# Second feed-forward's first projection by seven half-size products a chunk, with the seventh product's sum on GpSimd

## The reference

```python
def swiglu(h, w_in, w_out):
    gate, up = jnp.split(h @ w_in, 2, axis=-1)
    return ((jax.nn.silu(gate) * up) @ w_out).astype(h.dtype)
...
        h = h + swiglu(rms_norm(h, ffn_norm[i]), ffn_w_in[i], ffn_w_out[i])
    h = rms_norm(h, final_norm)
```

## Time and profile before

| | |
|---|---|
| median of 3 runs | 1679.61 us (1678.21 to 1684.54) |
| span of the profiled execution | 1680.7 us |
| the profiled execution's own time | not given apart from its span |
| TensorE busy | 1640.0 us, 98% |
| TensorE weight loads busy | 1333.0 us, 79% |
| VectorE busy | 919.1 us, 55% |
| ScalarE busy | 632.4 us, 38% |
| GpSimd busy | 92.6 us, 6% |
| chunks 1 to 21 of the second up-projection | about 1316 to 1545 us |
| down-projection behind it | about 1545 to 1666 us |

### The profile page before, as it was taken

How to read it: one execution, slowest core, us unless ns; L and a number is a source line. 1 busy time by engine, 2 the same in 40 slices (tenths; PEclk the granted TensorE clock), 3 DMA queues, 4 the chain that set the end, 5 groups by cost and what they waited for, 6 DMA issues and landing times.

```text
span 1680.7 us, 20208 instructions
## 1 busy us (share of the span) xinstructions
PE 1640.0 (98%) x7941; PEld 1333.0 (79%) x7941; DVE 919.1 (55%) x1262; ACT 632.4 (38%) x816; POOL 92.6 (6%) x130
## 2 busy tenths in 40 slices
PE   8999999999999999999999999999999999999997
PEld 3588777878887888888888789977768888888885
DVE  5665686677667654444444574145766544444323
ACT  2352458432233343333332533146653332223221
POOL 0100000111010000000000100003420000000000
PEclk9899999999999999999999999999999999999998
DMA  9432101755444233332234221224442333332331
GB/s 320 129 119 80 44 26 51 226 164 179 160 150 151 64 102 85 101 101 77 86 103 131 86 76 52 76 65 96 97 127 75 101 100 101 100 90 66 92 104 51
DMA packets 227365, 176.71 MB, mean 105 GB/s; under 512 B 15812, under 2 KB 213316, under 8 KB 227270
## 3 DMA queue, kind: packets, MB, share of 16 engines
q1 hardware_dynamic: 220662, 151.23, 30.9%
q0 software_dynamic: 6608, 24.19, 4.4%
HBM read 166.84 MB, written 2.13 MB: 101 GB/s over the span
## 4 chain that ended last, share of the span: by engine, by line
PE 83%; DVE 9%; ACT 4%; issue 1%; SPq 1%; DMA 1%; DVEq 0%; POOLq 0%; POOL 0%; ACTq 0%
PE PS L477 23%; PE PS L479 23%; PE PS L478 23%; PE PS L2393 2%; PE PS L486 1%; DVE WL L92 1%; DVE T L92 1%; DMA MODW<-in_w_mod 1%; PE PS L498 1%; PE PS L500 1%; PE PS L499 1%; SPq L2682 1%; PE PS L649 1%; ACT WH L88 1%; DVE SUMS L111 1%
## 5 line engine op out<-in xcount | busy, mean ns | idle before, releaser
L477 PE MATMUL PS<-XH,WH 128*128 128x512 f32 (+2 forms) x1264 | 481.1, 381 | 3.2 <-DVE WL L92 1.1
L478 PE MATMUL PS<-XL,WH 128*128 128x512 f32 (+2 forms) x1264 | 476.8, 377 | 0.0
L479 PE MATMUL PS<-XH,WL 128*128 128x512 f32 (+2 forms) x1264 | 476.8, 377 | 0.0
L92 DVE TENSOR_TENSOR WL<-WS,WH 128x2048 fp32r<-128x2048 f32 (+3 forms) x131 | 272.8, 2083 | 209.4 <-ACT WH L88 206.6
L477 PEld LDWEIGHTS PS<-XH,WH 128*128 128x128 f32 (+1 forms) x1264 | 236.0, 187 | 48.9 <-DVE WL L92 2.0
L479 PEld LDWEIGHTS PS<-XH,WL 128*128 128x128 f32 (+1 forms) x1264 | 235.9, 187 | 44.8
L478 PEld LDWEIGHTS PS<-XL,WH 128*128 128x128 f32 (+1 forms) x1264 | 236.0, 187 | 43.2 <-issue 0.7
L88 ACT ACTIVATE WH<-WS 128x2048 fp32r<-128x2048 f32 (+3 forms) x131 | 229.1, 1749 | 76.2 <-PE PS L479 46.7
L477 PE MATMUL PS<-HH,WH 128*128 128x512 f32 x352 | 137.2, 390 | 0.2 <-DVE WL L92 0.2
L478 PE MATMUL PS<-HL,WH 128*128 128x512 f32 x352 | 136.9, 389 | 0.0
L479 PE MATMUL PS<-HH,WL 128*128 128x512 f32 x352 | 136.9, 389 | 0.0
(11 more groups left out here) (373 smaller groups left out, 2294.7 us busy)
## 6 DMA issues: line engine op xcount, KB each, us to landing
WS<-in_w_in SPq DMA_DIRECT2D x24, 1024.0 KB, 5.4
WS<-in_ffn_w_up SPq DMA_DIRECT2D x44, 512.0 KB, 4.9
WS<-in_ffn_w_in SPq DMA_DIRECT2D x44, 512.0 KB, 4.8
MSRC<-in_w_mod POOLq DMA_DIRECT2D x32, 512.0 KB, 4.9
WS<-in_fox_w_in SPq DMA_DIRECT2D x16, 1024.0 KB, 5.6
WS<-in_ffn_w_down SPq DMA_DIRECT2D x16, 704.0 KB, 4.5
WS<-in_ffn_w_out SPq DMA_DIRECT2D x16, 704.0 KB, 4.5
MODW<-in_w_mod SPq DMA_DIRECT2D x8, 1024.0 KB, 11.7
```

What stands on the lines that cost most here:

```text
L92: self.e.tensor_tensor(o, a, b, op).then_inc(*self.done.to(*key))
L477: e.matmul(o, lh, rh, start=first and i == 0, stop=False)
L478: e.matmul(o, lh, rl, start=False, stop=False)
L479: ins = e.matmul(o, ll, rh, start=False, stop=last and i == n - 1)
```

## The change

Chunks 1 to 21 of the second up-projection are computed by Strassen's scheme in Winograd's form: the product of a 2 x 2 block matrix (4 row blocks by 256 tokens; 4 row blocks by 128 columns) by seven products of blocks in place of eight, with sums of blocks before and after. Chunk 0 keeps the old form.

- Weights: a chunk is loaded as two blocks (`blocks`) and turned into seven blocks of 512 columns, in four units (`unit`). Unit 0 (one block, 512 columns) and unit 3 (two) are taken from WS, units 1 and 2 from sums that GpSimd forms in SA or SB (`sums_pool`, four instructions of 512 columns a chunk, two chunks ahead). ScalarE makes the high halves (`hi_unit`), VectorE the low ones (`lo_unit`).
- Rows: three differences of halves of the rows, and a fourth that replaces a quarter of XH and XL after chunk 0, are formed by VectorE in `out2_dve` (`t_first_dve`, `t_third_dve`, `t_rest_dve`) with their high (`t_hi_act`) and low halves (`t_lo_dve`).
- Products: `up2_pe` makes parts 1, 6, 5, 7, 3, 4, 2 in this order, 12 matmuls of 256 columns each, into halves of PSUM banks; two sets of four banks alternate.
- Sums of products: ScalarE copies part 1, and parts 5 and 7 together, out of PSUM (`up2_copy`). VectorE adds part 6 (`up2_second_dve`), GpSimd makes three additions of 256 columns on the copies (`up2_pool`), VectorE adds parts 3 and 4, scales the gate half by RST, and adds part 2 (`up2_combined_dve`). The other half is not scaled by RST any more; the down-projection's result is.
- Room: X is written to HBM (`x_out`) and read back (`x_in`), and so are tiles 5 to 10 of HH and HL (`h_out`, `h_in`), since SB, UG and PC, and TSH and TSL, lie where X and the last six tiles of H were. Tiles 16 to 21 take the places of 5 to 10.
- `down2_pe`, `down2_act` and `down2_dve` replace `down_pe`, `down_act` and `down_dve` there, with one more VectorE instruction for each of 8 tiles.

The core of the diff:

```diff
+    def blocks(w, f):
+        return False, 8, 256, [(x, w[:, :, 2816 * (1 - x) + 128 * f:2816 * (1 - x) + 128 * f + 128]) for x in range(2)]
...
-    chunks += [pairs(u_in, f) for f in range(22)]
+    chunks += [blocks(u_in, f) for f in range(22)]
...
+    def lo_unit(v, f, b):
+        v.e.wait_ge(*acts.at("up2_wh", f, b))
+        v.tt(unit_cells(WL, f, b), unit_source(f, b), unit_cells(WH, f, b).bitcast(F32), ALU.subtract,
+             key=("up2_wl", f, b))
+        if b == 3:
+            dve.name("wl", UP2 + f)
...
+        if f > 1:
+            g.e.wait_ge(*dve.at("up2_wl", f - 1, b))
+        if b == 1:
+            g.tt(S[:, 1, :], st[:, 2, :], st[:, 3, :], ALU.add)
+            g.tt(S[:, 0, :], S[:, 1, :], st[:, 0, :], ALU.subtract, key=("up2_s", f, 1))
+        else:
+            g.tt(S[:, 2, :], st[:, 2, :], st[:, 0, :], ALU.subtract)
+            g.tt(S[:, 3, :], st[:, 1, :], S[:, 0, :], ALU.subtract, key=("up2_s", f, 2))
...
+        for f in range(1, 22):
+            e.wait_ge(*dve.at("up2_wl", f, 0))
+            if f > 2:
+                e.wait_ge(*dve.at("up2_c11", f - 2))
+            part_pe(e, f, 1)
+            e.wait_ge(*dve.at("up2_wl", f, 1))
...
+            part_pe(e, f, 6)
...
+            part_pe(e, f, 5)
+            e.wait_ge(*dve.at("up2_wl", f, 2))
+            part_pe(e, f, 7)
...
+            part_pe(e, f, 3)
+            e.wait_ge(*dve.at("up2_wl", f, 3))
...
+            part_pe(e, f, 4)
+            part_pe(e, f, 2)
+            pe.name("w", UP2 + f)
...
+    def up2_combined_dve(v, f):
+
+        e = v.e
+        e.wait_ge(*pe.at("up2", f, 4))
+        e.wait_ge(*pool.at("up2_t", f))
+        v.tt(UG[:, :, :].rearrange("p x n -> p (x n)")[:, 256:768], part_bank(f, 3, 512),
+             PC[:, 2:4, :].rearrange("p x n -> p (x n)"), ALU.add, key=("up2_cc", f))
+        e.wait_ge(*pool.at("up2_c22", f))
+        v.tt(up2_tile(f), UG[:, 1, :], RST[:, 0:L], ALU.mult, key=("up2_first", f))
+        e.wait_ge(*pe.at("up2", f, 2))
+        v.tt(UG[:, 0, 0:256], part_bank(f, 2), first_copy(f), ALU.add, key=("up2_c11", f))
...
+        for f in range(1, 22):
+            if f > 1:
+                up2_combined_dve(v, f - 1)
+            lo_unit(v, f, 3)
+            if f < 21:
+                lo_unit(v, f + 1, 0)
+            up2_second_dve(v, f)
+            if f > 1:
+                up2_times_dve(v, f - 1)
+            if f < 21:
+                lo_unit(v, f + 1, 1)
+            else:
+                lo_chunk(v, DN2)
...
+            up2_lo_dve(v, f - 1)
+            if f < 21:
+                lo_unit(v, f + 1, 2)
...
+        for f in range(1, 22):
+            e.wait_ge(*acts.at("up2_copy", f, 5))
+            e.wait_ge(*dve.at("up2_u2", f))
+            if f > 1:
+                e.wait_ge(*dve.at("up2_first", f - 1))
+            g.tt(PC[:, 3, :], PC[:, 3, :], PC[:, 0, :], ALU.add)
+            g.tt(UG[:, 1, 256:512], PC[:, 3, :], PC[:, 1, :], ALU.add, key=("up2_c22", f))
+            g.tt(PC[:, 2, :], PC[:, 0, :], PC[:, 1, :], ALU.add, key=("up2_t", f))
+            if f + 2 < 22:
+                sums_pool(g, f + 2, 1)
+                sums_pool(g, f + 2, 2)
...
+            v.tt(SQT[:, k % 2, :], bank((0, 1, 2, 7)[k % 4]), RST[:, 0:L], ALU.mult)
+            if k == 0:
+                v.e.wait_ge(*landed("x_in"))
+            v.tt(xk(k), xk(k), SQT[:, k % 2, :], ALU.add, key=("down2", "x", k))
...
             load_chunk(e, j)
+            if j == UP2 + 2:
+                park_load(e, "x_out")
+            if j == UP2 + 14:
+                park_load(e, "h_out")
+            if j == DN2 + 2:
+                park_load(e, "h_in")
+                park_load(e, "x_in")
```

More of the change, by code:

```diff
@@ L298, in build, with home, kept @@
     KO = zone("KO", [128, 8, L], F32R, 16)
+    TSH, TSL = (zone(n, [128, 3, 4, 256], F32R, k) for n, k in (("TSH", 32), ("TSL", 76)))
+    TS = zone("TS", [128, 4, 4, 256], F32, 60)
+    SA = zone("SA", [128, 4, 512], F32, 52)
+    SB = zone("SB", [128, 4, 512], F32, 88)
+    UG = zone("UG", [128, 2, 512], F32, 96)
+    PC = zone("PC", [128, 4, 256], F32, 100)
+    XPARK = nc.dram_tensor("xpark", (128, 8 * L), F32, kind="Internal").ap()
+    HPARK = [nc.dram_tensor(f"hpark{i}", (128, 6 * L), F32, kind="Internal").ap() for i in range(2)]
+    def home(f):
+        return f if f < 16 else f - 11
+    def kept(f):
+        return f + 11 if 5 <= f < 11 else home(f)
     A1, AC, A2, QG, FINV, G12, RV = 0, 8, 16, 32, 40, 48, 56
@@ L403, in load_chunk @@
             e.wait_ge(*dve.at("wl", j - 3))
+        if UP2 <= j < DN2:
+            view = stage(j).rearrange("p (x k n) -> p x k n", x=2, k=nk)
+            for x, src in parts:
+                e.dma_start(view[:, x, :, :], src).then_inc(ws_in[slot(j)], 16)
+            return
         view = stage(j).rearrange("p (k n) -> p k n", k=nk)
@@ L1774, in up_dve, with unit, sums_of, unit_source @@
                 meta_rest_dve(v)
+    UNIT_OF = {1: (0, 0), 6: (1, 0), 5: (1, 1), 7: (2, 0), 3: (2, 1), 4: (3, 1), 2: (3, 0)}
+    def unit(w, f, b):
+        p1 = place(UP2 + 1)
+        if b == 0:
+            return w[:, p1, 0:512] if f % 2 else w[:, p1, 1536:2048]
+        return (w[:, p1, 512:1536], w[:, 1 - p1, 0:1024], w[:, 1 - p1, 1024:2048])[b - 1]
+    def sums_of(f):
+        return SA if f == 1 else SB
+    def unit_source(f, b):
+        st = stage(UP2 + f)
+        if b == 0:
+            return st[:, 0:512]
+        if b == 3:
+            return st.rearrange("p (x n) -> p x n", x=2)[:, :, 512:1024]
+        return sums_of(f)[:, 2 * b - 2:2 * b, :].rearrange("p x n -> p (x n)")
@@ new lines, in unit_cells, with hi_unit @@
+    def unit_cells(w, f, b):
+        u = unit(w, f, b)
+        return u.rearrange("p (x n) -> p x n", x=2) if b == 3 else u
+    def hi_unit(a, f, b):
+        if b in (0, 3):
+            a.e.wait_ge(ws_in[slot(UP2 + f)], arrived[UP2 + f])
+        else:
+            a.e.wait_ge(*pool.at("up2_s", f, b))
+        if f == 1:
+            a.e.wait_ge(*pe.at("w", UP2 - 1 if b < 2 else UP2))
+        elif b == 0 and f > 2:
+            a.e.wait_ge(*pe.at("up2", f - 2, 1))
+        elif b:
+            a.e.wait_ge(*pe.at("up2", f - 1, (5, 3, 2)[b - 1]))
+        a.act(unit_cells(WH, f, b), unit_source(f, b), ACT.Copy, key=("up2_wh", f, b))
@@ new lines, in part_pe, with up2_pe @@
+    def part_pe(e, f, p):
+        b, x = UNIT_OF[p]
+        wh, wl = (unit(w, f, b)[:, 512 * x:512 * x + 512] for w in (WH, WL))
+        rh, rl = rows_of(p)
+        tm = [(wh[:, 128 * k:128 * k + 128], wl[:, 128 * k:128 * k + 128], rh[:, k, :], rl[:, k, :]) for k in range(4)]
+        prod(e, part_bank(f, p), tm, ("up2", f, p))
+    def up2_pe(e):
+        w, wl = (t[:, place(UP2), :].rearrange("p (x k n) -> p x k n", x=2, k=8) for t in (WH, WL))
+        e.wait_ge(*dve.at("wl", UP2))
+        tm = [terms(w[:, m], wl[:, m], 0) for m in range(2)]
+        prod_by_rows(e, [bank(1), bank(2)], tm, lambda k: dve.at("norm4", "lo", k), ("up2", 0))
+        e.wait_ge(*dve.at("norm4", "sum", 7))
+        pe.name("w", UP2)
+        sums_pe(e, "norm4", T[2], L, True, True, ("norm4", "sums"), step=1)
+        for f in range(1, 22):
[4 more added lines that the diff above has]
+            e.wait_ge(*dve.at("up2_wl", f, 1))
+            if f == 1:
+                e.wait_ge(*dve.at("t_lo", 3))
+            part_pe(e, f, 6)
+            if f == 2:
+                e.wait_ge(*dve.at("up2_times", 0))
+            part_pe(e, f, 5)
+            e.wait_ge(*dve.at("up2_wl", f, 2))
+            part_pe(e, f, 7)
+            if f == 1:
+                spread_pe(e, "norm4", L)
+            part_pe(e, f, 3)
+            e.wait_ge(*dve.at("up2_wl", f, 3))
+            if f == 1:
+                e.wait_ge(*dve.at("t_fourth"))
+            part_pe(e, f, 4)
+            part_pe(e, f, 2)
+            pe.name("w", UP2 + f)
@@ new lines, in up2_copy @@
+    def up2_copy(a, f, p):
+        a.e.wait_ge(*pe.at("up2", f, {1: 6, 5: 7}[p]))
+        if p == 1 and f > 2:
+            a.e.wait_ge(*dve.at("up2_c11", f - 2))
+        elif p == 5 and f > 1:
+            a.e.wait_ge(*pool.at("up2_t", f - 1))
+            a.e.wait_ge(*dve.at("up2_cc", f - 1))
+        elif p == 5:
+            a.e.wait_ge(*landed("x_out"))
+        if p == 1:
+            a.act(first_copy(f), part_bank(f, 1), ACT.Copy, key=("up2_copy", f, 1))
+        else:
+            a.act(PC[:, 1:4:2, :], part_bank(f, 5, 512).rearrange("p (x n) -> p x n", x=2), ACT.Copy,
+                  key=("up2_copy", f, 5))
@@ new lines, in first_copy, with up2_tile, up2_silu_act, up2_hi_act @@
+    def first_copy(f):
+        return T[0][:, 256 * (f % 2):256 * (f % 2) + 256]
+    def up2_tile(f):
+        return T[1 + f % 2][:, :]
+    def up2_silu_act(a, f):
+        a.e.wait_ge(*dve.at("up2_first", f))
+        a.act(up2_tile(f), up2_tile(f), ACT.Silu, key=("up2_silu", f))
+    def up2_hi_act(a, f):
+        a.e.wait_ge(*dve.at("up2_times", f))
+        if f == 16:
```

(65 more changed lines are left out.)

127 lines of the change are left out of this document (119 added, 8 removed).

## The result

The changed kernel took 1710.15 us (median of 4 runs, 1707.66 to 1713.2) against 1678.91 us (4 runs): a ratio of 1.0174, 95% interval 1.0147 to 1.0201. So it is slower, by more than the noise. The forecast was 1717, slower, with a range of 1696 to 1738. The profiled execution has a span of 1705.9 us and a time of 1707.66 us of its own.

What follows compares the result with a forecast made beforehand. The prediction took TensorE, busy throughout the stage, to bound the kernel. Its terms summed to 1680.7 - 21.2 + 52.8 - 2 + 4.5 + 2.5 + 0.7 = 1718.0 us of span, forecast as 1717, range 1696 to 1738.

Steps and rivals of the forecast that it cites:

- TensorE's part: Chunks 1 to 21: 84 matmuls of 256 columns take 9.87 us a chunk, 1.01 less; -21.2 us in all.
- exclusion: 19 chunks: VectorE's two-SBUF-input and GpSimd's instructions pass singly, 12.65 us a chunk; +52.8 us, less 2 us for lead.
- start: Before the stage and at chunk 1: VectorE's added row instructions and late first GpSimd sums delay TensorE, +4.5 us.
- parked tiles: Down-projection: TensorE waits for six tiles of H returning from HBM behind a weight load, +2.5 us.
- tail: Behind the last matmul: the root scaling moved into the down-projection adds one VectorE instruction, +0.7 us.
- (a): Changed stage: no collision that counts, TensorE's 9.87 us a chunk stands; 1664.6 us, faster; chance 0.12.
- (b): Changed stage: cheaper additions and more hidden by PSUM reads, 11.2 us a chunk; about even, 1680 us; chance 0.04.
- (c): Changed stage: VectorE and GpSimd exclude each other for whole instructions, 13.75 us a chunk; 1738 us; chance 0.08.
- (d): Changed stage: TensorE's clock falls to its lower level after its waits, +19 us; 1736 us; chance 0.10.

Runs made afterwards that it cites:

- E1: Changed kernel with each GpSimd addition of the stage replaced by two fills that only write, sums left out (wrong result): 1666.62 us, ratio 0.9923 to the kernel before.
- E2: Changed kernel without GpSimd's four 512-column sums from chunk 3 on, its three small additions kept (wrong result): 1686.19 us, ratio 1.002 to the kernel before.
- E5: Changed kernel with all three additions of products moved from GpSimd to VectorE, GpSimd keeping the four sums: 1722.98 us, ratio 1.0238 to the kernel before.
- E6: Changed kernel with one of GpSimd's four 512-column sums moved to VectorE from chunk 3 on: 1717.38 us, ratio 1.0203 to the kernel before.
- E4: Changed kernel with the seventh product's sum moved from GpSimd to VectorE, which reads it from PSUM: 1725.51 us, ratio 1.0269 to the kernel before.
- E3: Changed kernel with GpSimd's three additions cut to 8 of 256 columns from chunk 2 on (wrong result): 1690.23 us, ratio 1.0075 to the kernel before.

## Why the prediction was right, and where its sizes were off

The steps, with the term forecast and the term measured, from the end of the output projection to the end of the span (before 376.6 us, after 408.8, so +32.2; the forecast's sum was +37.3):

| step | forecast | measured |
|---|---|---|
| TensorE's part, 21 chunks | -21.2 | 21 x (10.88 - 10.08) = -16.8 |
| exclusion, 19 chunks | +52.8 - 2 | 19 x (11.89 - 10.08) = +34.4 |
| first chunk, and what is left of the stage's +21.4 | none | +3.8 |
| start | +4.5 | +6.4 |
| parked tiles and the rest of the down-projection | +2.5 | +3.7 |
| tail | +0.7 | +0.7 |

The forecast of 1717 was 7 us from the median, and its sum 5.1 us from this stretch. That is closer than its terms were, and partly luck: exclusion was put 16.4 us too high, while TensorE's gain (4.4), the first chunk (3.8), the start (1.9) and the tiles (1.2) were missed to the other side. Of the 16.4, 19 x 0.21 = 4.0 are TensorE's error counted once more, with the other sign, since in these chunks VectorE sets the pace.

*TensorE's part.* The pitch is 0.120 us in E1, where nothing disturbs it (13 starts from 1429.75 to 1431.19 in its timeline, 12 steps in 1.44), not the 0.1175 of the earlier trace rows, and its weight loads are busy all of the 10.08 us. A gain of 0.80 a chunk, not 1.01. Why the pitch is longer here, no run shows. In the chunks that collide, TensorE idles 11.85 - 10.08 = 1.8 us, where 2.78 was forecast, and it waits for two blocks, not three.

*Exclusion.* The mechanism was right, and so nearly was its floor, 11.9 us (5.54 + 6.43 = 11.97 unrounded, 0.12 above the steady cadence of 11.85). The mean is (1552.66 - 1338.69) / 18 = 11.89, between the additions of product 6 of chunks 2 and 20:

```profile
1338.69 0.42 DVE L92 TENSOR_TENSOR PC<-PS,T 128x256 f32<-128x256 f32 x1
...
1552.66 0.42 DVE L92 TENSOR_TENSOR PC<-PS,T 128x256 f32<-128x256 f32 x1
```

What was mis-sized is "at the end u2 itself with its gap and the request, 0.8 us in which GpSimd waits for u2 and nobody holds the pass". In the trace GpSimd's last sum (1432.54 to 1434.17) lies across u2 (1433.15 to 1433.57). In the steady cycle GpSimd runs late by one instruction and doesn't wait for u2, so the only PSUM read that I left uncovered is covered. 19 x (12.65 - 11.89) = 14 us of the forecast was that. GpSimd caught up with u2 only at 1339 and 1494 us, where it waited 1.24 us each time. The chunk before the second took 13.20 us, its scaling behind two sums (1.80 us in place of 0.78), and the one behind each wait 11.5. In E2 and E5, where GpSimd isn't saturated, the sum of exclusion (7.4 and 10.1 us) doesn't give the cadence (10.37 and 12.38), and VectorE's queue in its order does.

*Start.* I had put the delay at chunk 1; 1.39 us of it come before chunk 0. Its low halves wait for ScalarE's high halves (1.36 us), and these stand in ScalarE's queue behind the high halves of a row difference, which VectorE had just made. VectorE's added instructions are 20, not 16: 16 differences and 4 low halves; the 11 us forecast for them holds. The clock below was not forecast.

*Rivals.* (a) would have needed a sum and a split to fit beside each other, and they don't: its premise is false. Once GpSimd doesn't read (E1), the stretch from the output projection on is 10.6 us shorter than before, where its sum has 15.0; the 4.4 between them is the size of TensorE's error (21 x 0.21). That its time (1664.6, measured 1666.62) is met more closely is luck. (b), 11.2 a chunk, falls with the cadence of 11.85. (c), the whole instruction, falls: 13.75 a chunk was not seen. The rule of the Trainium skill named in the prediction ("SBUF — State Buffer", "Who interferes with whom") also says that a VectorE instruction with two SBUF inputs doesn't contend with a GpSimd one that only writes; E1 agrees, 1.225 us beside fills of 0.527 us. (d) came once in the changed kernel, at the start. In E6 it came eight times in the stage (granted clock 0.94 from 1330 to 1530 us, against 1.00 in the changed kernel), and even there VectorE's queue alone adds up to the cadence.

## What to carry to other kernels

Before work is handed to an idle engine, add up what both engines need of what they share, not only what each needs alone: here 8.0 and 7.3 us fitted into 10 one by one, and took 11.85 together. In these runs a VectorE instruction with both inputs in SBUF and a GpSimd one that reads added up; one that reads PSUM did not (0.69 and 0.42 us either way). An order that puts those beside GpSimd's instructions suggests itself, but no run tried a new order alone. What bounded this pair of in-order engines was VectorE's queue with its collisions: moving an instruction across (E4, E5, E6) lengthened its cycle each time (12.57, 12.38 and 12.29 us), even where it made the sum of exclusion smaller.

## What the runs showed of the hardware

After TensorE's wait of 4.85 us before chunk 1 the granted clock stood near its lower level, 1.2 of 2.4 GHz, for most of the next 5 us. Start to end, length, busy time, granted clock:

```profile
1310.00:1315.00 5.00, 0.48 (x5) 0.77 0.53 210
1315.00:1320.00 5.00, 4.67 (x23) 0.54 0.99 298
1320.00:1325.00 5.00, 5.00 (x39) 1.00 0.69 180
```

At 0.54 some 5 x 0.46 = 2.3 of those 5 us are lost (an estimate from these rows), more than half of the 3.8 us in the table. In the changed kernel waits of 0.75 and 0.52 us, one of each a chunk, left the clock at 1.00 (1400 to 1550 us).

In E6 TensorE waits once a chunk, and there the clock did fall, eight times. Behind a wait of 1.95 us that ended at 1413.01 it stayed at 1.00; behind the next one, also of 1.95, that ended at 1425.30, it fell for about 4 us:

```profile
1424.00:1426.00 2.00, 0.70 (x6) 1.00 0.00 0
1426.00:1428.00 2.00, 2.00 (x12) 0.53 0.64 173
1428.00:1430.00 2.00, 2.00 (x12) 0.61 1.17 332
1430.00:1432.00 2.00, 2.00 (x19) 1.00 0.12 27
```

TensorE's wait in the chunk behind is 0.47 us, so the slow stretch used up time that it would have waited. The cadence stays at 12.28 to 12.31 us through it.

An addition of 8 columns is not free: in E3 GpSimd's took 0.44, 1.25 and 0.72 us, started beside VectorE's instructions, and the sum of 512 columns behind them 2.25.
